# Block products of a chunked recurrence whose backward items write to the other partition half

## The chip, the cores and the metric

One core of a Trainium2 chip runs the whole program as one launch. The metric is the device time of that launch in microseconds (us); smaller is better. Everything is computed in float32.

## The reference

The reference is a two-part network: a first block of two layers (neighbourhood attention, a recurrent mixer, a convolution, then a dense or an expert feed-forward) and a second block of two layers. The change touches one thing in it, the recurrent mixer of the first block. It is computed for 512 tokens, in both directions, with four heads of 64 features. For each head and direction it holds a state matrix `X` (64 x 64) and goes through the tokens:

```
for each token t:   X <- diag(decay_t) X  +  b_t (z_t^T X)  +  k_t v_t^T        (delta-rule update)
                    y_t = X^T r_t                                              (output)
```

The kernel computes it in chunks of 64 tokens. In a chunk the update is a triangular system `(I - L) U = right-hand side`, where `L` (64 x 64, strictly triangular) holds products of the z and b rows. Its inverse is built from matrix products only: the part of `L` inside 16 x 16 blocks, `D`, gives the block inverse `E = (I + D)(I + D^2)(I + D^4)(I + D^8)`, as E1 = I + D, E2 = E1 + D^2 E1, E3 = E2 + D^4 E2, E4 = E3 + D^8 E3. The rest of `L` then gives N = E L', N^2, and `G = (I + N)(I + N^2)`, so that the system is solved by applying E and then G.

## The kernel before, in words

**Data layout.** SBUF and PSUM have 128 partitions; a 64 x 64 matrix fills one half, partitions 0 to 63 or 64 to 127 (`hs`, line 1500). Heads come in two pairs (`hp`), the two heads of a pair in the two halves. With two directions (`d`, 0 forward, 1 backward) and two chunk steps (`j`) a buffer such as `E`, `DD`, `LL`, `D4` holds 8 items side by side, each 64 columns, in both halves: index `i = 4 j + 2 d + hp`. PE's array is used as four quarters of 64 x 64: a matmul reads its operands from one half and writes to one half, so a quarter is a pair (half read, half written).

**A block product** (`products`, lines 1536 to 1541) goes over the 8 items and the two halves and reads and writes the same half. It uses only the two quarters on the diagonal. It is 16 matmuls; each shows in the trace as two pairs of a weight load (PEld) and a matmul, 32 pairs. Other matmuls (`against_zr`, `turned`, `rhs`, `state`, `outputs`) already write backward items to the other half (`time_half`, line 1543), since the backward direction keeps time in the other half.

**Order of the work.** A layer has NG = 4 groups of two chunks. All engines have the order of a group written out by hand, and count steps on three semaphores (`P_`, `V_`, `A_` for PE, VectorE and ScalarE, with the names in the lists of lines 1489 to 1499). In group g the inverse of g is built, in the products p1 to p7, and between them PE does the steps of the group before (s = g - 1): right-hand side (`rhs`), applying E (`solve_blocks`, line 1613), applying G (`solve`, 1618), state update (`state`, 1623) and outputs (`outputs`, 1634), once for each j. Lines 1657 to 1739 are PE's order:

- `dl`, `zb`: L and its transpose (1665, 1671 to 1672), then `rhs(s, 0)`.
- p1 (1677 to 1679): D^2 and its transpose. Then E applied (`w0`), and `kb0` (1683), key products for j = 0.
- p2 (1687 to 1689): D^4, its transpose, D^2 E. Then G applied (`u0`), `kb1` (1693).
- p3 (1697 to 1699): D^8, and D^4 E after E2 is there. Then the state update for j = 0.
- p4 (1705): D^8 E. Then outputs for j = 0 and `rhs(s, 1)`.
- p5 (1712, 1713): N transposed and N. Then `w1`.
- p6 (1722): N^2, then `u1`. p7 (1728): the last product. Then `state(s, 1)`.
- `bs`, `ks`, `vs` (1732, 1733, 1738): transposes by an identity (`turned`, line 1561; matmul at 1566), `outputs(s, 1)`.

ScalarE (lines 1820 to 1855) copies one result of each step out of PSUM (`out`, line 1790, instruction 1792; `rhs_out` 1796, `blocks_out` 1800, `solved` 1804). VectorE (lines 1934 to 1981) masks, copies (line 1913) and adds (line 1910) the others: `e2`, `e3`, `e4` are adds of a PSUM bank to E. Between them it does `taps.some`, multiply-adds of a convolution (line 735) that belong to another mixer and fill its time. `keys_out` (1901) masks the key products `km0`, `km1` (line 1907).

In layer 1 the first two groups need no outputs (`seen`, line 1479), so they have fewer products and narrower ones. In groups 0 and 1 of layer 0 and group 0 of layer 1 `fill_pe` places small matmuls of another part (lines 505 and 522) between the steps. After the fourth group a tail (1740 to 1786) does the steps of that group.

Of the kernel before, what the change touches and what calls it, by code (L numbers as in the profile page):

```python
# [14 lines left out]
P = 128  # L15
# [15 lines left out]
CH = 64  # L31
# [130 lines left out]
def build(nc, parts, xt_in, ct_in, con_in, par1_in, par2_in, lora_in, gate2_in, router_in, bias_in,  # L162
# [1066 lines left out]
    def recurrence(l, us, at, taps, mod, mod_done, mod_here):  # L1229
# [243 lines left out]
        dirs = lambda x: x.rearrange("p (j d hp) t -> p d j (hp t)", j=2, d=2)  # L1473
        step4 = lambda x: x.rearrange("p (d hp) t -> p d (hp t)", d=2)
# [14 lines left out]
        for g in range(NG):  # L1489
            tags_of(pn, ("dl", "zb", "old0", "rhs0", "p1", "w0", "kb0", "p2", "u0", "kb1", "p3", "dx0", "p4", "yx0", "y0", "old1",  # L1490
                         "rhs1", "p5", "w1", "p6", "u1", "p7", "dx1", "bs", "ks", "yx1", "y1", "vs"), g)
            tags_of(vn, ("d", "dt0", "dt1", "l", "e1", "mb0", "mb1", "d2", "km0", "d4", "e2", "km1", "e3", "xa0", "xb0",
                         "e4", "nt", "int", "g", "xa1", "xb1"), g)
            tags_of(an, ("rhs0", "d2t", "w0", "d4t", "u0", "d8", "ya0", "yb0", "rhs1", "n", "w1", "n2", "u1", "bs", "ks", "ya1", "yb1", "vs"), g)
# [26 lines left out]
        def _(pe):  # L1521
# [14 lines left out]
            def products(out, left, right):  # L1536

                for i in range(8):
                    for h in hs:
                        mm = pe.matmul(out[h, i, :], left[h, i, :], right[h, i, :], start=True, stop=True)  # L1540
                return mm
# [65 lines left out]
            def apply(name, region, left, s, j):  # L1607
                for hp, d, q in items():
                    for h in hs:
                        mm = pe.matmul(bank(5 + d)[h, spot(d, region, hp)], left[h, 4 * j + q, :], RH[h, q, :], start=True, stop=True)  # L1610
                mm.then_inc(P_.h, P_.one(f"{name}{j}_{s}"))

            def solve_blocks(s, j):
                pe.wait_ge(V_.h, V_.at(f"e4_{s}"))
                pe.wait_ge(A_.h, A_.at(f"rhs{j}_{s}"))
                apply("w", BLOCKS, E[s % 2], s, j)

            def solve(s, j):
                pe.wait_ge(V_.h, V_.at(f"g_{s}"))
                pe.wait_ge(A_.h, A_.at(f"w{j}_{s}"))  # L1620
                apply("u", RHS_U, GG_, s, j)
# [35 lines left out]
            for g in range(NG):  # L1657
# [54 lines left out]
                products(b8(0), LL, E[g % 2])  # L1712
                products(b8(1), E[g % 2], LL).then_inc(P_.h, P_.one(f"p5_{g}"))
# [4 lines left out]
                pe.wait_ge(V_.h, V_.at(f"km1_{g}"))  # L1718
                pe.wait_ge(A_.h, A_.at(f"n_{g}"))
                if g and seen(s):  # L1720
                    pe.wait_ge(A_.h, A_.at(f"yb0_{s}"))
                products(b8(3), NTb, N1).then_inc(P_.h, P_.one(f"p6_{g}"))
# [66 lines left out]
        def _(act):  # L1789
# [3 lines left out]

            def rhs_out(s, j):
                act.wait_ge(P_.h, P_.at(f"rhs{j}_{s}"))
                act.activation(step4(RH), near(5, RHS_U), ACT.Copy).then_inc(A_.h, A_.one(f"rhs{j}_{s}"))
# [23 lines left out]
            for g in range(NG):  # L1820
# [8 lines left out]
                out("d4t", "p2", g, 1, D4T)  # L1829
# [3 lines left out]
                out("d8", "p3", g, 0, D8)  # L1833
# [5 lines left out]
                out("n", "p5", g, 1, N1)  # L1839
# [3 lines left out]
                out("n2", "p6", g, 3, N2)  # L1843
# [46 lines left out]
        def _(dve):  # L1890
# [4 lines left out]
            of_dir = lambda x, d: x.rearrange("p (j d hp) t -> p d j hp t", j=2, d=2)[:, d]  # L1895
            of_step = lambda x, j, rows: x.rearrange("p (j d hp) w t -> p j d hp (w t)", j=2, d=2)[:, j, :, :, 0:rows * CH]
# [37 lines left out]
            for g in range(NG):  # L1934
                s, rows, e = g - 1, 2 if seen(g) else 1, E[g % 2]
                after(f"dl_{g}")
                mult(dirs(DD), grams, wide("mask_d"), f"d_{g}")
                after(f"zb_{g}")
                for d in range(2):
                    mult(of_dir(DT, d), zr_of(d)[:, :, :, 0, :], per_dir(mdt, d), f"dt{d}_{g}")  # L1940
                mult(dirs(LL), grams, wide("mask_l"), f"l_{g}")
# [11 lines left out]
                copy(D4, b8(0), f"d4_{g}")  # L1953
                add(e, b8(2), e, f"e2_{g}")
# [11 lines left out]
                add(e, b8(2), e, f"e4_{g}")  # L1966
                taps.some(dve, 1)
                after(f"p5_{g}")
                copy(NTb, b8(0), f"nt_{g}")
                add(INT_, b8(0), eye, f"int_{g}")  # L1970
# [1816 lines left out]
```

## Time and profile before

| | before |
|---|---|
| median of 3 runs | 2932.83 us (2929.32 to 2934.77) |
| span of the profiled execution | 2929.3 us |
| PE / PE weight load / VectorE / ScalarE / GpSimd busy | 94% / 78% / 66% / 51% / 3% |
| recurrence, layer 0 (four groups) | about 288.7 to 399 us |
| recurrence, layer 1 (four groups) | about 1064.7 to 1169 us |

The profile gives for every group of instructions the engine, the line of the kernel, the operation and its busy time. PE stands for matmuls, PEld for the weight loads that overlap them, DVE for VectorE, ACT for ScalarE, PEclk for the granted clock as a share of 2.4 GHz. A view by stretches lists for each engine the busy time and, in brackets, the instructions: PE, PEld, DVE, ACT, POOL. In a timeline, neighbouring instructions of the same kind are merged into one row (start, duration of the whole, count), and rows of one engine may overlap by the last instruction's duration. The idle time before a row and its releaser stand in brackets; the releaser "issue" is idle time for which the profile shows no cause. The page gives the span of the execution that was profiled and no other time for it; its span lies at the low end of the three runs.

### The profile page before, as it was taken

To read this page: it belongs to the slowest core of one execution; us is meant where nothing else is said; L and a number is where in the kernel's file an instruction comes from. 1 tells how busy PE (TensorE), PEld (TensorE's weight loads), DVE (VectorE), ACT (ScalarE), POOL (GpSimd) and SP (SyncE) were. 2 spreads that over 40 slices of the span, in tenths; PEclk is the share of its full clock that TensorE was granted. 3 is DMA by queue.
4 is the path that set the end of the run, shared out by engine and by line. 5 is a ranking of instruction groups with operands and counts; after the bars stand their busy time and mean duration, and the time that the engine had idled before them with its cause. 6 is when DMAs were issued, how large, how long until landed. Compare 5 with 4: busy or idle time off the path is not lost.

```text
span 2929.3 us, 50739 instructions
## 1 busy us (share of the span) xinstructions
PE 2739.9 (94%) x21324; PEld 2299.2 (78%) x21324; DVE 1943.8 (66%) x2283; ACT 1481.0 (51%) x1753; POOL 101.6 (3%) x79
## 2 busy tenths in 40 slices
PE   6998888999999978799999999999999889989999
PEld 4875776888768767778778787877877779987999
DVE  3365775322454567578888888888888657665766
ACT  3344243222433433367677777777776445443544
POOL 1100000000012000010000000000000000000000
PEclk9998999999999989899999999999999889998999
DMA  8514101322234230089899898989996424542453
GB/s 318 220 58 172 69 3 62 111 101 87 101 130 155 76 138 4 13 335 373 335 354 348 333 367 336 371 336 349 366 346 258 162 101 175 186 147 87 158 187 117
DMA packets 81796, 581.69 MB, mean 199 GB/s; under 512 B 9272, under 2 KB 11072, under 8 KB 11840
## 3 DMA queue, kind: packets, MB, share of 16 engines
q1 hardware_dynamic: 78336, 571.48, 51.6%
q10 hardware_dynamic: 3264, 7.33, 0.7%
q8 instruction: 155, 2.54, 0.3%
q14 instruction: 41, 0.34, 0.0%
HBM read 577.73 MB, written 1.05 MB: 198 GB/s over the span
## 4 chain that ended last, share of the span: by engine, by line
PE 82%; DVE 8%; ACT 4%; PEld 2%; issue 1%; DMA 1%; PEldq 1%; POOL 0%; POOLq 0%; ACTq 0%; DVEq 0%; SPq 0%
PE banks L2496 20%; PE banks L2520 11%; PE banks L2834 9%; PE banks L1077 8%; PE banks L857 8%; PE banks L1103 3%; PE banks L891 3%; PE banks L1540 3%; PE banks L3160 3%; PEld banks L679 1%; DVE ring_split L307 1%; PE banks L2088 1%; DVE ring_split L2673 1%; PE banks L522 1%; DVE x_buf L2662 1%
## 5 line engine op out<-in xcount | busy, mean ns | idle before, releaser
L2673 DVE TENSOR_TENSOR ring_split<-ring,arena_split 128x2048 fp32r<-128x2048 f32 x336 | 768.3, 2291 | 90.8 <-ACT arena_split L2601 82.6
L2601 ACT ACTIVATE arena_split<-ring 128x2048 fp32r<-128x2048 f32 x336 | 644.3, 1918 | 52.3 <-PE banks L2520 52.2
L307 DVE TENSOR_TENSOR ring_split<-ring,arena_split 128x2048 fp32r<-128x2048 f32 x144 | 339.6, 2360 | 338.0 <-ACT arena_split L301 338.0
L301 ACT ACTIVATE arena_split<-ring 128x2048 fp32r<-128x2048 f32 x144 | 274.4, 1908 | 103.8 <-PE banks L1077 74.0
L2496 PE MATMUL banks<-arena_split 128*128 128x512 f32 x896 | 301.5, 399 | 11.7 <-DVE ring_split L2673 11.7
L2496 PE MATMUL banks<-arena_split,mix_split 128*128 128x512 f32 x896 | 304.1, 401 | 6.4 <-DVE ring_split L2673 6.4
L2520 PE MATMUL banks<-arena_split 128*128 128x512 f32 x896 | 297.2, 392 | 1.0 <-DVE arena_split L2702 1.0
L2496 PEld LDWEIGHTS banks<-arena_split 128*128 128x128 f32 x896 | 169.6, 189 | 49.0 <-DVE ring_split L2673 13.4
L2496 PEld LDWEIGHTS banks<-arena_split,mix_split 128*128 128x128 f32 x896 | 168.3, 188 | 45.0 <-DVE ring_split L2673 8.3
L2520 PEld LDWEIGHTS banks<-arena_split 128*128 128x128 f32 x896 | 168.2, 188 | 43.2 <-issue 4.4
L857 PE MATMUL banks<-mix_split,ring_split 128*128 128x256 f32 x704 | 198.8, 282 | 0.0
L857 PE MATMUL banks<-h_split,arena_split 128*128 128x256 f32 x704 | 197.6, 281 | 0.0
L857 PE MATMUL banks<-mix_split,arena_split 128*128 128x256 f32 x704 | 196.8, 279 | 0.2
L2496 PE MATMUL banks<-ring_split,arena_split 128*128 128x512 f32 x448 | 176.9, 395 | 0.0
L2520 PE MATMUL banks<-ring_split,arena_split 128*128 128x512 f32 x448 | 175.9, 393 | 0.0
L2496 PE MATMUL banks<-ring_split,mix_split 128*128 128x512 f32 x448 | 175.5, 392 | 0.0
L2834 PE MATMUL banks<-mix_split,arena_split 128*128 128x512 f32 (+1 forms) x352 | 138.0, 392 | 11.0 <-DVE h_split L450 9.6
L1077 PE MATMUL banks<-mix_split,arena_split 128*128 128x512 f32 x352 | 139.7, 397 | 7.2 <-DVE h_split L450 7.2
L1077 PE MATMUL banks<-h_split,arena_split 128*128 128x512 f32 x352 | 138.8, 394 | 0.0
L1077 PE MATMUL banks<-mix_split,ring_split 128*128 128x512 f32 x352 | 138.2, 393 | 0.0
L857 PEld LDWEIGHTS banks<-mix_split,arena_split 128*128 128x128 f32 x704 | 132.6, 188 | 2.2 <-issue 1.5
L2834 PE MATMUL banks<-h_split,arena_split 128*128 128x512 f32 (+1 forms) x352 | 132.8, 377 | 0.0
(408 smaller groups left out, 5447.5 us busy)
## 6 DMA issues: line engine op xcount, KB each, us to landing
ring<-parts SPq DMA_DIRECT2D x541, 1024.0 KB, 4.8
arena<-bias ACTq DMA_DIRECT2D x2, 2048.0 KB, 9.5
x_buf<-xt SPq DMA_DIRECT2D x1, 2048.0 KB, 7.8
constants<-con SPq DMA_DIRECT2D x1, 1952.0 KB, 14.5
out<-x_buf ACTq DMA_DIRECT2D x4, 256.0 KB, 2.2
arena<-lora ACTq DMA_DIRECT2D x2, 256.0 KB, 3.4
arena<-gate ACTq DMA_DIRECT2D x2, 256.0 KB, 3.6
arena<-sgw ACTq DMA_DIRECT2D x2, 256.0 KB
```

The source lines that it names most:

```text
L301: act.activation(high[:, m % depth, :], slots[:, n % RING, :], ACT.Copy).then_inc(w_high.h, w_high.one(times))
L307: dve.tensor_tensor(low_slots[:, n % RING, :], slots[:, n % RING, :], high[:, m % high.shape[1], :].bitcast(F32), ALU.subtract).then_inc(w ...
L857: mm = pe.matmul(bk[:, j * 256:(j + 1) * 256], w[:, k, j * P:(j + 1) * P], x[:, k, c0:c0 + 256], start=k == 0 and n == 0, stop=k == KT - 1 ...
L891: mm = pe.matmul(y(t), w[:, j, t * P:(t + 1) * P], h[:, U % 2, j * 256:(j + 1) * 256], start=False, stop=False, skip_group_check=True)
L1077: mm = pe.matmul(o, w[:, k, j * P:(j + 1) * P], x[:, k, :], start=k == 0 and n == 0, stop=k == KT - 1 and n == 2)
L1103: mm = pe.matmul(bank(4 * p + t), w[:, e % 4, c], h[b], start=k == 0 and n == 0, stop=k == n_hid - 1 and n == 2)
L1540: mm = pe.matmul(out[h, i, :], left[h, i, :], right[h, i, :], start=True, stop=True)
L2496: mm = pe.matmul(pair_bank(U), x[:, k, at], w[:, j, :], start=k == 0 and g == 0, stop=k == KT - 1 and g == 2)
L2520: mm = pe.matmul(bank(4 + half), h[:, U % 2, j * P:(j + 1) * P], w[:, j, half * 512:(half + 1) * 512], start=times == 1 and u == 0 and j = ...
L2601: act.activation(high[:, m % 3, :], slots[:, m % RING, :], ACT.Copy).then_inc(wh_ok.h, 1)
L2673: dve.tensor_tensor(low_slots[:, m % RING, :], slots[:, m % RING, :], high[:, m % 3, :].bitcast(F32), ALU.subtract).then_inc(wl_ok.h, 1)
L2834: mm = pe.matmul(o, left, right, start=kk == 0 and n == 0, stop=kk == KT - 1 and n == 2)
```

## The change

Seven of the twelve block products of a group (D^4, its transpose, D^8, N, its transpose, and the two that make E2 and E3) are done by a new function `crossed`. Forward items stay in their half; backward items write to the other half, and forward and backward items go to two neighbouring PSUM banks. The items in the buffers are ordered by direction first (`4 d + 2 j + hp`). For E2 and E3 the sum with E is formed in PSUM by a second matmul with an identity (`plus=True`), since E must move to the other half as well; VectorE then copies instead of adding. D crosses at D^4 and again at D^8, E at E2 and again at E3, so p4 is again an uncrossed product. N and its transpose cross once, so p6 and p7 are uncrossed products of crossed items, and G lies crossed. Applying E crosses the backward items over, applying G crosses them back.

In the order of work `kb1` moves from behind `u0` to behind the state update of j = 0, and waits for the copy of D^8; VectorE's `km1` moves behind `e3` and that state update; PE's waits for `km1` and for the outputs' copy move from p6 to p5; D^4's transpose comes last in p2 and waits for `km0`.

```diff
+        pair = lambda b, k: by_dir(b, b + 2)[:, :, k * 256:(k + 1) * 256].rearrange("p d (i t) -> p d i t", i=4)
+        pair_like = lambda x: x.rearrange("p (d i) t -> p d i t", d=2)
...
+            def crossed(b, k, left, right, plus=False):
+
+                o = [bank(b + d)[:, k * 256:(k + 1) * 256].rearrange("p (i t) -> p i t", i=4) for d in range(2)]
+                for i in range(4):
+                    for w in range(2 if plus else 1):
+                        for d in range(2):
+                            for h in hs:
+                                to = hs[1 - hs.index(h)] if d else h
+                                mm = pe.matmul(o[d][to, i, :], eye[h, 0, :] if w else left[h, 4 * d + i, :], right[h, 4 * d + i, :],
+                                               start=w == 0, stop=w == int(plus))
                 return mm
...
-            def apply(name, region, left, s, j):
+            def apply(name, region, left, s, j, from_crossed):
                 for hp, d, q in items():
                     for h in hs:
-                        mm = pe.matmul(bank(5 + d)[h, spot(d, region, hp)], left[h, 4 * j + q, :], RH[h, q, :], start=True, stop=True)
+                        of, to = (time_half(h, q), h) if from_crossed else (h, time_half(h, q))
+                        mm = pe.matmul(bank(5 + d)[to, spot(d, region, hp)], left[of, 4 * d + 2 * j + hp, :], RH[of, q, :],
+                                       start=True, stop=True)
...
-                products(b8(0), D2T, D2)
-                products(b8(1), D2, D2T)
-                products(b8(2), D2, E[g % 2]).then_inc(P_.h, P_.one(f"p2_{g}"))
+                crossed(0, 0, D2T, D2)
+                crossed(0, 1, D2, E[g % 2], plus=True)
+                pe.wait_ge(V_.h, V_.at(f"km0_{g}"))
+                crossed(2, 0, D2, D2T).then_inc(P_.h, P_.one(f"p2_{g}"))
                 if g:
                     solve(s, 0)
-                pe.wait_ge(V_.h, V_.at(f"km0_{g}"))
-                against_zr(kt, g, 1).then_inc(P_.h, P_.one(f"kb1_{g}"))
...
-                products(b8(0), D4T, D4)
+                crossed(2, 0, D4T, D4)
                 pe.wait_ge(V_.h, V_.at(f"e2_{g}"))
-                products(b8(1), D4, E[g % 2]).then_inc(P_.h, P_.one(f"p3_{g}"))
+                crossed(0, 0, D4, E[g % 2], plus=True).then_inc(P_.h, P_.one(f"p3_{g}"))
                 if g:
                     state(s, 0)
+                pe.wait_ge(A_.h, A_.at(f"d8_{g}"))
+                against_zr(kt, g, 1).then_inc(P_.h, P_.one(f"kb1_{g}"))
...
-                products(b8(2), D8, E[g % 2]).then_inc(P_.h, P_.one(f"p4_{g}"))
+                products(b8(0), D8, E[g % 2]).then_inc(P_.h, P_.one(f"p4_{g}"))
...
                 pe.wait_ge(V_.h, V_.at(f"e4_{g}"))
-                products(b8(0), LL, E[g % 2])
-                products(b8(1), E[g % 2], LL).then_inc(P_.h, P_.one(f"p5_{g}"))
+                if g and seen(s):
+                    pe.wait_ge(A_.h, A_.at(f"yb0_{s}"))
+                pe.wait_ge(V_.h, V_.at(f"km1_{g}"))
+                crossed(2, 0, LL, E[g % 2])
+                crossed(0, 0, E[g % 2], LL).then_inc(P_.h, P_.one(f"p5_{g}"))
...
-                copy(D4, b8(0), f"d4_{g}")
-                add(e, b8(2), e, f"e2_{g}")
+                copy(pair_like(D4), pair(0, 0), f"d4_{g}")
+                copy(pair_like(e), pair(0, 1), f"e2_{g}")
+                taps.some(dve, 1)
+                after(f"p3_{g}")
+                copy(pair_like(e), pair(0, 0), f"e3_{g}")
+                if g:
+                    state(s, 0)
                 after(f"kb1_{g}")
                 keys_out(g, 1, rows)
                 taps.some(dve, 1)
-                after(f"p3_{g}")
-                own()
-                add(e, b8(1), e, f"e3_{g}")
-                if g:
-                    state(s, 0)
-                taps.some(dve, 1)
```

## Rows read from the trace of the kernel before

**Rows 1.** The page: span, busy times, PE's instruction queue, shares of the chain by line.

```profile
span 2929.3 us, 50739 instructions
PE 2739.9 (94%) x21324; PEld 2299.2 (78%) x21324; DVE 1943.8 (66%) x2283; ACT 1481.0 (51%) x1753; POOL 101.6 (3%) x79
...
q8 instruction: 155, 2.54, 0.3%
...
PE banks L2496 20%; PE banks L2520 11%; PE banks L2834 9%; PE banks L1077 8%; PE banks L857 8%; PE banks L1103 3%; PE banks L891 3%; PE banks L1540 3%; PE banks L3160 3%; PEld banks L679 1%; DVE ring_split L307 1%; PE banks L2088 1%; DVE ring_split L2673 1%; PE banks L522 1%; DVE x_buf L2662 1%
```

**Rows 2.** Stretches: length, then busy us (count) by engine, clock, DMA share, GB/s.

```profile
317.60:344.60 27.00, 24.31 (x868) 22.78 (x868) 23.01 (x48) 7.35 (x18) 0.00 (x0) 0.98 0.02 4
344.60:371.30 26.70, 24.26 (x916) 22.98 (x918) 22.24 (x40) 9.28 (x20) 0.00 (x0) 1.00 0.02 5
1091.30:1114.70 23.40, 20.46 (x768) 19.22 (x768) 16.84 (x38) 6.68 (x15) 0.00 (x0) 1.00 0.02 5
```

**Rows 3.** Timeline of group 1 of layer 0, p2 to p4.

```profile
323.39 2.88 PEld L1540 LDWEIGHTS banks<-arena 64*64 64x64 f32 x96
...
323.61 1.41 DVE L735 SCALAR_TENSOR_TENSOR mix_buf<-arena,par,mix_buf 128x512 f32<-128x512 f32 x2
...
326.18 0.55 PEld L1610 LDWEIGHTS banks<-arena 64*64 64x64 f32 x16
...
326.45 0.69 DVE L1913 COPY arena<-banks 128x512 f32<-128x512 f32 x1 [1.44 <-PE banks L1540]
...
327.06 0.68 DVE L1910 TENSOR_TENSOR arena<-banks,arena 128x512 f32<-128x512 f32 x1
327.20 1.95 PEld L1540 LDWEIGHTS banks<-arena 64*64 64x64 f32 x64
...
330.32 1.01 PEld L1540 LDWEIGHTS banks<-arena 64*64 64x64 f32 x32 [0.71 <-DVE arena L1910]
...
330.83 0.49 DVE L1930 TENSOR_TENSOR arena<-arena 128x128 f32<-128x128 f32 x2
...
331.25 0.55 PEld L1641 LDWEIGHTS banks<-arena 64*64 64x64 f32 x16
```

**Rows 4.** Stops named "issue": timeline, stretches between stops, and the queues from 343.48.

```profile
339.84 0.13 PEld L1630 LDWEIGHTS banks<-arena 64*64 64x64 f32 x1 [0.24 <-issue]
339.85 1.06 PEld L1566 LDWEIGHTS banks<-constants,h_buf 64*64 64x64 f32 x64
...
343.49 0.21 PEld L1566 LDWEIGHTS banks<-constants,arena 64*64 64x64 f32 x8 [1.17 <-issue]
...
369.71 0.21 PEld L1665 LDWEIGHTS banks<-h_buf,arena 64*64 64x64 f32 x8 [0.86 <-issue]
...
339.83:343.48 3.65, 2.55 (x128) 2.27 (x127) 3.48 (x8) 1.53 (x4) 0.00 (x0) 1.00 0.03 7
366.36:369.70 3.34, 2.56 (x130) 2.27 (x127) 3.25 (x7) 2.30 (x6) 0.00 (x0) 1.00 0.02 5
1164.97:1169.05 4.08, 2.77 (x127) 2.38 (x126) 1.28 (x4) 3.15 (x6) 0.00 (x0) 1.00 0.01 4
343.48:369.70 26.22, 23.70 (x888) 22.28 (x888) 22.97 (x48) 8.20 (x20) 0.00 (x0) 1.00 0.02 4
...
q8 instruction: 7, 0.11, 1.8%
```

**Rows 5.** Timeline of the same group: an operation on four quarters.

```profile
332.46 0.33 PEld L1588 LDWEIGHTS banks<-arena 64*64 64x64 f32 x16
```

**Rows 6.** First groups: two stops (timeline), then both groups by stretches.

```profile
301.52 0.66 PEld L1540 LDWEIGHTS banks<-arena 64*64 64x64 f32 x19 [1.31 <-issue]
...
314.42 0.20 PEld L1566 LDWEIGHTS banks<-constants,h_buf 64*64 64x64 f32 x6 [2.72 <-issue]
...
288.70:317.60 28.90, 21.48 (x648) 18.20 (x652) 20.44 (x34) 5.16 (x9) 0.00 (x0) 0.96 0.57 230
1064.67:1091.30 26.63, 21.09 (x612) 19.88 (x612) 15.75 (x36) 4.53 (x8) 0.00 (x0) 0.81 0.12 51
```

More of the change, by code:

```diff
@@ L1489, in recurrence @@
         for g in range(NG):
-            tags_of(pn, ("dl", "zb", "old0", "rhs0", "p1", "w0", "kb0", "p2", "u0", "kb1", "p3", "dx0", "p4", "yx0", "y0", "old1",
+            tags_of(pn, ("dl", "zb", "old0", "rhs0", "p1", "w0", "kb0", "p2", "u0", "p3", "dx0", "kb1", "p4", "yx0", "y0", "old1",
                          "rhs1", "p5", "w1", "p6", "u1", "p7", "dx1", "bs", "ks", "yx1", "y1", "vs"), g)
-            tags_of(vn, ("d", "dt0", "dt1", "l", "e1", "mb0", "mb1", "d2", "km0", "d4", "e2", "km1", "e3", "xa0", "xb0",
+            tags_of(vn, ("d", "dt0", "dt1", "l", "e1", "mb0", "mb1", "d2", "km0", "d4", "e2", "e3", "xa0", "xb0", "km1",
                          "e4", "nt", "int", "g", "xa1", "xb1"), g)
@@ L1620, in solve @@
                 pe.wait_ge(A_.h, A_.at(f"w{j}_{s}"))
-                apply("u", RHS_U, GG_, s, j)
+                apply("u", RHS_U, GG_, s, j, True)
             def state(s, j):
@@ L1717, in _ @@
                 pe.wait_ge(V_.h, V_.at(f"nt_{g}"))
-                pe.wait_ge(V_.h, V_.at(f"km1_{g}"))
                 pe.wait_ge(A_.h, A_.at(f"n_{g}"))
-                if g and seen(s):
-                    pe.wait_ge(A_.h, A_.at(f"yb0_{s}"))
-                products(b8(3), NTb, N1).then_inc(P_.h, P_.one(f"p6_{g}"))
+                products(b8(4), NTb, N1).then_inc(P_.h, P_.one(f"p6_{g}"))
                 if g:
@@ L1792, in out, with pair_out @@
                 act.activation(o, b8(b), ACT.Copy).then_inc(A_.h, A_.one(f"{name}_{g}"))
+            def pair_out(name, of, g, b, o):
+                act.wait_ge(P_.h, P_.at(f"{of}_{g}"))
+                act.activation(pair_like(o), pair(b, 0), ACT.Copy).then_inc(A_.h, A_.one(f"{name}_{g}"))
             def rhs_out(s, j):
@@ L1828, in _ @@
                 fill_act(act, g, "p1")
-                out("d4t", "p2", g, 1, D4T)
+                pair_out("d4t", "p2", g, 2, D4T)
                 if g:
@@ L1832, in _ @@
                 fill_act(act, g, "p2")
-                out("d8", "p3", g, 0, D8)
+                pair_out("d8", "p3", g, 2, D8)
                 fill_act(act, g, "p3")
@@ L1838, in _ @@
                 fill_act(act, g, "p4")
-                out("n", "p5", g, 1, N1)
+                pair_out("n", "p5", g, 0, N1)
                 if g:
@@ L1842, in _ @@
                 fill_act(act, g, "p5")
-                out("n2", "p6", g, 3, N2)
+                out("n2", "p6", g, 4, N2)
                 if g:
@@ L1936, in _ @@
                 after(f"dl_{g}")
-                mult(dirs(DD), grams, wide("mask_d"), f"d_{g}")
+                mult(own_dirs(DD), grams, wide("mask_d"), f"d_{g}")
                 after(f"zb_{g}")
                 for d in range(2):
-                    mult(of_dir(DT, d), zr_of(d)[:, :, :, 0, :], per_dir(mdt, d), f"dt{d}_{g}")
-                mult(dirs(LL), grams, wide("mask_l"), f"l_{g}")
+                    mult(own_dir(DT, d), zr_of(d)[:, :, :, 0, :], per_dir(mdt, d), f"dt{d}_{g}")
+                mult(own_dirs(LL), grams, wide("mask_l"), f"l_{g}")
                 own()
@@ L1957, in _ @@
                 taps.some(dve, 1)
-                after(f"p3_{g}")
-                own()
-                add(e, b8(1), e, f"e3_{g}")
-                if g:
-                    state(s, 0)
-                taps.some(dve, 1)
                 after(f"p4_{g}")
                 own()
-                add(e, b8(2), e, f"e4_{g}")
+                add(e, b8(0), e, f"e4_{g}")
                 taps.some(dve, 1)
                 after(f"p5_{g}")
-                copy(NTb, b8(0), f"nt_{g}")
-                add(INT_, b8(0), eye, f"int_{g}")
+                copy(pair_like(NTb), pair(2, 0), f"nt_{g}")
+                add(pair_like(INT_), pair(2, 0), eye_pair, f"int_{g}")
                 taps.some(dve, 2)
```

6 lines of the change are left out of this document (5 added, 1 removed).

## The prediction

> **What bounds the kernel now.** The page's shares come first: TensorE (PE) is busy 94% of the span, and the chain that ended last runs over its lines; the block products of line 1540 are 3% of it, some 88 us [rows 1]. So a shorter PE stage here can shorten the kernel, unless another wait takes its place. The busy time by stretches shows two full groups of layer 0 at 27.0 and 26.7 us and one of layer 1 at 23.4 us; in layer 0 PE is busy 24.3 us of a group and VectorE (DVE) 22 to 23 us [rows 2] (the second stretch ends inside the next group, so it counts more loads). DVE is a close second, so not all that PE saves can show. There are eight groups, four in each layer.
>
> The timeline of one group of layer 0 is the next view [rows 3]. The reader is to see three kinds of piece: products that PE runs back to back (96 weight loads from 323.39, and the next line starts at 326.18), waits for a copy to land (0.71 us before p4 at 330.32), and DVE's convolution taps, each pair 1.41 us, which sit between the copies.
>
> The last view decides this forecast: stops of PE whose releaser is "issue", that is nothing the profile shows. There is one of 0.24 us before 339.84 and one of 1.17 us before 343.49 [rows 4]. Between the two PE ran 127 pairs of a weight load and a matmul and took 3.65 us, though it was busy only 2.3 to 2.6 us. From 366.37 to 369.71 it is 127 pairs again and 3.34 us, ending in a stop of 0.86 us, and in layer 1 126 pairs and 4.08 us [rows 4]. From stop to stop, 343.49 to 369.71, there are 888 pairs, one short of 7 times 127, and the instruction queue q8 moved 7 packets [rows 4]; its packets are 2.54 MB over 155, 16.4 KB each [rows 1]. I read this so: one packet carries some 256 PE instructions (127 pairs, two instructions each, and the waits among them), and a new packet serves PE every 3.34 to 4.08 us at best, mostly 3.4 to 3.6. I take 3.5 us, or 27 ns for a pair. A product on two quarters issues at 2.79/96 = 29 ns for a pair [rows 3], just under that ceiling, which is why only the stretches at the end of a group hit it.
>
> **The change part by part.**
>
> *Five plain crossed products* (D4, D4T, D8, N, NT). A product is 16 matmuls, 32 pairs in the trace. On two quarters it takes 0.93 us (2.79/3) [rows 3]. On all four the trace has another operation with the same shape and the same order over directions and halves, line 1566: 64 loads in 1.06 us, of which the last lasts 0.13, so 14.7 ns a pair and 0.47 us for 32 [rows 4]. That saves 0.46 each, 2.3 a group.
>
> *Two crossed products with E added on PE* (E2, E3): 64 pairs at 14.7 ns, 0.94 us, against 0.93. Nothing saved, but 64 more pairs a group. DVE's add becomes a copy of the same size: 0.68 us against 0.69 [rows 3], nothing.
>
> *Applying the inverse,* four times a group: 16 pairs in 0.55 us now (line 1610), 0.33 us where four quarters are used (line 1588) [rows 3, 5]. That is 0.2 each, 0.8 a group.
>
> So PE's own work falls by 3.1 us a group, about 24 us in all. How much shows, if instructions are always there, I walk along the group. p2: 128 pairs, 1.87 us against 2.79, gain 0.9; DVE is done with km0 and its taps at 325.02, before the product would land, so nothing takes that back. The way to p3: before, solve and kb1 cover the copy of D4 (326.18 to 327.20, 1.02 us); after, kb1 is gone from there but PE waits for the copy all the same, gain 0. D8 takes 0.47, but E3 must wait for the copy of E2, 0.61 behind that of D4: 0.3 gained of 0.46. p4: E3's copy no longer queues behind km1 and taps, so the wait of 0.71 us before p4 [rows 3] shrinks to 0.4, gain 0.3; kb1 (16 pairs, 0.4 us) fits into that wait, its new wait for d8 included. But km1 now stands on DVE behind e3 and the state update (0.69, some 0.4 for an add of half the size, 0.49 and 0.69 us), and the outputs and the right-hand side queued on PE wait for it: 0.5 lost. p5: 0.93 gained, less 0.15 since nt then comes behind two taps. p6, p7 and the turned products: nothing; their moved waits (km1, yb0) are done by then. Together 1.8 us a group, **14 us** in all. No transfer, SyncE or GpSimd step is moved.
>
> *Instructions.* The same trace says they are not always there. A layer 0 group has 864 pairs (868 loads in the window less 4 of another line [rows 2]) and would have 928. With some 18 waits in the code that is 7.3 packets, 25.6 us at 3.5 each, against 26.9 measured; in layer 1's first groups 768 pairs become 832, 6.6 packets, 23.0 us against 23.4. So even with no other wait the eight groups could gain only 5 us. And packets are not evenly used. From p2 to the end of p4 the new order wants 128+16+96+32+16+32 = 320 pairs, 2.5 packets or 8.75 us; a packet that lies ready at its start makes up part of it, and I take 8.4. Now it is 7.86 us (323.39 to 331.25). That is 0.5 slower where the walk above had gained 1.0. The km1 wait costs nothing here, since PE stands in the same place for instructions. The rest of the group keeps about 0.7 of its 0.8, as the stop at its end (1.17 us before 343.49) only starts earlier. Net 0.2 a group: **−1.4 us**.
>
> *The first group of layer 0* runs while weights stream in (DMA share 0.57 [rows 6]); its stops for instructions are 1.31 and 2.72 us [rows 6], so a packet takes longer there, some 5 us. 64 more pairs are half a packet: between 0 and +2.8 us on top, and I take **+2.5**, since all its long stops are of this kind.
>
> *The tail* of each layer has four applies with ScalarE between them: 0.2 each where PE is late, at most 1.6 over both layers; half of it lies beside convolution work. **−0.6**.
>
> Sum: −1.4 + 2.5 − 0.6 = +0.5 us. The profiled execution spans 2929.3 us; the runs shown are 2929.32 to 2934.77, median 2932.83, so the profile is 0.12% under the median. I forecast **2933.3 us**, no change that can be told (0.2%, 5.9 us, is about what a measurement of this kernel can tell).
>
> Now two rules of the Trainium skill. The rows show PE stopped for up to 1.17 us at exact multiples of 256 instructions with almost no other DMA about [rows 4]. "Runtime: NRT & Kernel Launch", Instruction fetch mechanics, says blocks of 256 instructions are refilled ahead, and that fetching is hidden because instructions issue more slowly than they arrive. The block size agrees with the trace; the hiding does not. By that rule the sum would be rival 1's. "TensorE: Matmul & The Clock Gate", section "Wait — 56ns, not 53.3ns?", says starts of matmuls never come closer than about 25 ns however small they are. By that rule crossing gains next to nothing and the added pairs cost in full, rival 3; the trace has 14.7 ns.
>
> **The rivals.**
>
> *Rival 1: instructions keep up.* Then the 14 us of the walk and 0.6 of the tail show: 2932.8 − 14.6 = **2918.2 us**. For it: most of the 256-instruction blocks pass without a stop today. Against it: they do so at 29 ns a pair, and all dense stretches at 15 ns show a stop or a thinning. A ceiling of 3.3 us rather than 3.5 gives half of it, about −5.
>
> *Rival 2: the ceiling is lower than I take it,* in the stretch from p2 to p4. Price: at 3.8 us a packet it takes 2.5 × 3.8 = 9.5 less what lies ready, 9.1, so 1.2 us more than now, of which 0.5 comes back later; with eight groups and the first one's 2.5 it is +8, **2941 us**. It decides from about 3.6 us a packet. For it: the 3.65 and 4.08 us intervals; against: 3.34.
>
> *Rival 3: crossed products do not overlap* as line 1566 does, since there one operand is a constant. At 29 ns a pair the two long products cost 0.93 more each, and nothing is gained: 8 × 1.9 = +15, **2948 us**. Against it: line 1588 multiplies data by data and reaches 0.33 us for 16 pairs [rows 5].
>
> **How the numbers follow.** The forecast, instructions as the ceiling near 3.5: 0.62. Rival 1 with its halfway case 0.17; rival 2: 0.17; rival 3: 0.04. Faster by over 0.2% takes rival 1 and the edge of the forecast, 0.18; slower by over 0.2% takes rivals 2 and 3 and its other edge, 0.22; within, 0.60. The range runs from 2921 us, which holds the halfway case and part of rival 1, to 2942 us, rival 2's end; the ends beyond hold under 0.2. PE's clock is at the upper level (1.00) in the full groups and lower in the first group of layer 1 (0.81 [rows 6]); I see nothing that moves it, and 1 us either way is inside the range.
>
> **What would show it.** Right: plain crossed products at about 15 ns a pair; "issue" stops inside p3, p4 and p5 of nearly every group, at distances of 256 PE instructions and 3.4 to 3.7 us; about 4 more packets on q8 in all; groups of 26.5 and 23 us; PEld counts 64 higher a group. Wrong: groups of 25 and 21 us with no new stop (rival 1); intervals of 3.8 us and more (rival 2); 29 ns a pair on the new line (rival 3); or PE waits for km1 before the outputs larger than 0.5 us with instructions at hand.

## The result and the profile after

The changed kernel takes 2940.47 us (median of 20 runs, 2934.3 to 2947.77), beside 2932.75 for the kernel before in the same comparison (20 runs, 2920.94 to 2938.67). The ratio is 1.0026, 95% interval 1.0018 to 1.0034. That is 7.7 us slower, just more than the 0.2% bound, while PE's busy time fell by 10.9 us.

First the page of the changed kernel: span, busy times, PE's instruction queue, the chain by engine.

```profile
span 2943.7 us, 51759 instructions
...
PE 2729.0 (93%) x21836; PEld 2282.7 (78%) x21836; DVE 1941.7 (66%) x2283; ACT 1480.5 (50%) x1753; POOL 101.4 (3%) x79
...
q8 instruction: 159, 2.61, 0.4%
...
PE 82%; DVE 8%; ACT 4%; issue 2%; PEld 2%; DMA 1%; PEldq 1%; POOL 0%; POOLq 0%; ACTq 0%; DVEq 0%; SPq 0%
```

Against [rows 1] there are 512 more pairs of a weight load and a matmul, 64 in each of eight groups, and q8 moved 159 packets where it moved 155. DVE and ScalarE do what they did. The profiled execution is one of the slower ones (2943.7 us, 14.4 over the profile of before, where the medians differ by 7.7), so lengths are read stage by stage.

The first three groups of each layer, from group start to group start, by the same columns as [rows 2]:

```profile
289.21:316.66 27.45, 20.22 (x673) 16.33 (x676) 19.33 (x33) 4.45 (x8) 0.00 (x0) 0.88 0.61 242
316.66:345.52 28.86, 22.86 (x947) 21.17 (x942) 23.54 (x42) 7.53 (x18) 0.00 (x0) 0.94 0.02 4
345.52:371.82 26.30, 21.48 (x941) 19.45 (x937) 21.74 (x47) 7.08 (x17) 0.00 (x0) 1.00 0.02 4
1073.15:1095.94 22.79, 16.92 (x641) 15.63 (x645) 15.29 (x32) 4.07 (x7) 0.00 (x0) 0.85 0.09 34
1095.94:1119.77 23.83, 17.43 (x848) 16.24 (x843) 16.66 (x41) 6.64 (x14) 0.00 (x0) 1.00 0.02 4
1119.77:1145.32 25.55, 19.32 (x847) 17.33 (x841) 18.70 (x41) 6.53 (x14) 0.00 (x0) 1.00 0.02 4
```

And the same six in the kernel before, cut at the same places of the code:

```profile
288.70:316.33 27.63, 20.21 (x609) 17.04 (x612) 20.44 (x34) 4.57 (x8) 0.00 (x0) 0.98 0.59 240
316.33:343.72 27.39, 24.78 (x878) 23.28 (x875) 22.20 (x40) 7.43 (x18) 0.00 (x0) 0.96 0.02 4
343.72:368.63 24.91, 23.11 (x878) 21.83 (x874) 21.66 (x47) 7.14 (x17) 0.00 (x0) 1.00 0.02 5
1064.67:1090.52 25.85, 20.35 (x577) 19.29 (x580) 15.19 (x32) 4.07 (x7) 0.00 (x0) 0.80 0.13 53
1090.52:1113.70 23.18, 20.47 (x784) 19.23 (x779) 16.39 (x40) 6.54 (x14) 0.00 (x0) 1.00 0.02 5
1113.70:1137.35 23.65, 21.12 (x783) 19.90 (x777) 18.45 (x41) 6.54 (x14) 0.00 (x0) 1.00 0.02 4
```

The reader is to see two things. In the four full groups PE is busy 1.6 to 3.0 us less and the group is 0.65 to 1.9 us longer: what PE no longer works, it waits. And the first groups did not get slower. The end of the recurrence is marked in the timeline by the first reciprocal behind it, first in the changed kernel, then in the kernel before:

```profile
435.79 0.20 DVE L2209 RECIPROCAL arena<-arena 128x8 f32<-128x8 f32 x1 [1.20 <-ACT arena L2168]
...
1201.29 0.18 DVE L2209 RECIPROCAL arena<-arena 128x4 f32<-128x4 f32 x1 [0.58 <-ACT arena L2168]
```

```profile
429.01 0.20 DVE L2186 RECIPROCAL arena<-arena 128x8 f32<-128x8 f32 x1 [1.20 <-ACT arena L2145]
...
1191.60 0.18 DVE L2186 RECIPROCAL arena<-arena 128x4 f32<-128x4 f32 x1 [0.58 <-ACT arena L2145]
```

From the last group's start to there it is 63.97 us against 60.38 in layer 0 and 55.97 against 54.25 in layer 1. Together: +5.4 in the full groups, −3.2 in the first ones, +5.3 in the last ones with the tail, so +7.5 us inside the recurrence; the other 6.9 us of this execution lie outside, where the code is the same. This is near the difference of the medians, but it is no proof, since single executions differ too. The traces of e4 and e6 below, whose medians cannot be told from the kernel before's, have 2.9 and 4.3 us more than this trace of before in the same four full groups, and e6 has 64.16 us from the last group's start of layer 0 to the reciprocal. The medians and the experiments carry the verdict; the traces show where the time goes.

Where in a group? The stretch from the first weight load of p2 to the end of p4, in the four full groups of the changed kernel:

```profile
325.14:333.16 8.02, 6.58 (x321) 5.99 (x321) 6.50 (x13) 1.47 (x3) 0.00 (x0) 1.00 0.02 4
351.65:360.67 9.02, 6.64 (x320) 6.01 (x321) 7.59 (x14) 1.60 (x4) 0.00 (x0) 1.00 0.01 4
1101.44:1110.73 9.29, 5.80 (x320) 5.52 (x320) 5.14 (x13) 1.70 (x4) 0.00 (x0) 1.00 0.02 5
1125.68:1135.24 9.56, 6.62 (x319) 5.90 (x320) 6.34 (x14) 1.59 (x4) 0.00 (x0) 1.00 0.02 3
```

It holds the 320 pairs forecast and takes 8.97 us on the mean, of which PE is busy 6.4. Before, the same stretch was 7.86, 7.85, 7.76 and 7.76 us with 256 pairs. The timeline of group 2 of layer 0 shows what fills the rest:

```profile
356.20 0.26 PEld L1554 LDWEIGHTS banks<-arena 64*64 64x64 f32 x11 [0.73 <-issue]
...
360.03 0.71 PEld L1543 LDWEIGHTS banks<-arena 64*64 64x64 f32 x21 [0.99 <-issue]
...
364.07 0.67 PEld L1554 LDWEIGHTS banks<-arena 64*64 64x64 f32 x40 [0.86 <-issue]
```

Three stops for instructions in a row, 3.83 and 4.04 us apart; the stretches between them hold 129 and 127 pairs. Beside them PE waits for copies, 0.70 us before 354.93 and 0.38 before 358.18. In [rows 4] such stops stood at the end of a group; now they stand inside it as well. Counted in 256 instructions, eight blocks start from 345.28 to 371.01, and five of them start with an "issue" stop. From 323.81 to 372.22 the packets on q8 start 3.72 us apart on the mean.

The added identity pairs are no dearer for the array than the others. At the start of the same stretch in group 1 they alternate with products, eight pairs each, and eight start every 0.11 to 0.12 us, 15 ns a pair:

```profile
325.72 0.21 PEld L1554 LDWEIGHTS banks<-arena,constants 64*64 64x64 f32 x8
325.84 0.21 PEld L1554 LDWEIGHTS banks<-arena 64*64 64x64 f32 x8
325.95 0.21 PEld L1554 LDWEIGHTS banks<-arena,constants 64*64 64x64 f32 x8
```

### The profile page after: what moved, and what is told of

Its sections match the earlier page's. It is cut to its first block, busy times and chain, and to the rows that moved or that the text cites. A ratio compares the mean times of both kernels' runs of the same rounds, so it can differ in the third digit from the quotient of the medians.

```text
span 2943.7 us, 51759 instructions
## 1 busy us (share of the span) xinstructions
PE 2729.0 (93%) x21836; PEld 2282.7 (78%) x21836; DVE 1941.7 (66%) x2283; ACT 1480.5 (50%) x1753; POOL 101.4 (3%) x79
## 3 DMA queue, kind: packets, MB, share of 16 engines
HBM read 577.73 MB, written 1.05 MB: 197 GB/s over the span
## 4 chain that ended last, share of the span: by engine, by line
PE 82%; DVE 8%; ACT 4%; issue 2%; PEld 2%; DMA 1%; PEldq 1%; POOL 0%; POOLq 0%; ACTq 0%; DVEq 0%; SPq 0%
PE banks L2519 20%; PE banks L2543 11%; PE banks L2857 9%; PE banks L1077 8%; PE banks L857 8%; PE banks L1103 3%; PE banks L891 3%; PE banks L3183 3%; PE banks L1543 2%; PE banks L1554 1%; PE banks L2111 1%; PEld banks L679 1%; DVE ring_split L307 1%; DVE ring_split L2696 1%; PE banks L522 1%
```

## The experiments

Times are medians, ratios are against the kernel before on the same chip with their 95% intervals. In these comparisons the kernel before has 2935.0 to 2937.9 us, not 2932.75, so differences and ratios are to be compared with the expectations, not their absolute times. "Instruction theory": PE is given a block of 256 instructions, 127 or 128 pairs, every 3.5 to 4 us at best, and what it does in its quarters matters only beyond that. "Array theory": the quarters and the waits for copies set the time.

**e1: the same instructions on two quarters.** In the changed kernel:

```diff
-                                to = hs[1 - hs.index(h)] if d else h
+                                to = h
...
-                        of, to = (time_half(h, q), h) if from_crossed else (h, time_half(h, q))
+                        of, to = h, h
```

> The changed kernel with every crossed matmul and both applies written to the half they are read from, so that only two quarters are used; number and order of PE instructions, copies and waits are the changed kernel's. What is computed for backward items of the recurrence is another thing. Instruction theory (256 PE instructions are served every 3.7 us, 29 ns a pair, whatever the quarters): a two-quarter pair costs 29 ns, just what the instructions allow, so this is only a little slower than the changed kernel, +2 to +8 us (2942 to 2949). Array theory (the crossing pays in full, and the loss lies in the moved waits): PE's own work grows by 14 ns on 160 pairs of plain products, 128 of E2 and E3 and 64 of the applies, 5.0 us a group: +25 to +40 us against the changed kernel.

Measured: 2952.88 us, ratio 1.0051 (1.0037 to 1.0066). That is some 7 us over the changed kernel, inside what the instruction theory allowed (+2 to +8) and far from the array theory's +25 to +40. Taking the four quarters away costs only 7 us although PE's busy time rises by 32 (2761.0 us). Where the expectation speaks of other sums, it is wrong: every item stays in its half, and the sums are complete.

**e2: without the identity products.**

```diff
-                crossed(0, 1, D2, E[g % 2], plus=True)
+                crossed(0, 1, D2, E[g % 2])
...
-                crossed(0, 0, D4, E[g % 2], plus=True).then_inc(P_.h, P_.one(f"p3_{g}"))
+                crossed(0, 0, D4, E[g % 2]).then_inc(P_.h, P_.one(f"p3_{g}"))
```

> The changed kernel without the 32 identity matmuls a group (64 pairs, 128 PE instructions) that add E to D^2 E and D^4 E; E is left out of these sums, all else as in the changed kernel. Instruction theory: half a packet less a group, 1.9 us, so -12 to -15 us against the changed kernel: 2926 to 2929, below the kernel before. Array theory: 64 pairs at 14.7 ns, 0.94 us a group, at most -7.5 us: 2933 or more.

Measured: 2923.89 us, ratio 0.9958 (0.9943 to 0.9973), so 12 us under the kernel before. E is left out of the sums E2 and E3. Two full groups, one of each layer:

```profile
314.79:340.33 25.54, 21.46 (x879) 19.76 (x875) 21.94 (x39) 7.53 (x18) 0.00 (x0) 0.95 0.02 5
...
1088.01:1109.91 21.90, 18.14 (x780) 16.92 (x775) 16.10 (x36) 6.54 (x14) 0.00 (x0) 0.91 0.02 5
```

The instruction theory had −12 to −15 for the group's 64 pairs against the changed kernel, the array theory at most −7.5; it is −20 (12 under the kernel before, which the changed one is 8 over). So both were too low, and the 64 pairs cost at least what they cost as instructions. What makes the other 5 us is not shown.

**e3: only N, its transpose and the applies cross.** The order and the products up to p4 are those of the kernel before; nothing is added on PE.

```diff
-                crossed(0, 0, D2T, D2)
-                crossed(0, 1, D2, E[g % 2], plus=True)
-                pe.wait_ge(V_.h, V_.at(f"km0_{g}"))
-                crossed(2, 0, D2, D2T).then_inc(P_.h, P_.one(f"p2_{g}"))
+                products(b8(0), D2T, D2)
+                products(b8(1), D2, D2T)
+                products(b8(2), D2, E[g % 2]).then_inc(P_.h, P_.one(f"p2_{g}"))
...
                 crossed(2, 0, LL, E[g % 2])
                 crossed(0, 0, E[g % 2], LL).then_inc(P_.h, P_.one(f"p5_{g}"))
```

> Only N, its transpose and the applies of the inverse cross; p2, p3, p4 and the order of kb1 and km1 are those of the kernel before. As many PE instructions as before; PE's own work falls by 0.9 us a group in p5 and 0.8 in the applies. Instruction theory: the kernel before already averages one packet in 3.75 us, so the stops at the group's end grow by nearly as much as the products shrink: 0 to -4 us against the kernel before (2929 to 2933). Array theory: 1.2 us a group beyond waits show: -8 to -10 us (2923 to 2925).

Measured: 2926.51 us, ratio 0.9966 (0.9955 to 0.9978), 10 us faster than the kernel before. Here the array theory (−8 to −10) was right and the instruction theory (0 to −4) wrong: the blocks of the kernel before are not all full of pairs at 29 ns, some are long because of their work and waits, and there shorter work shows. The two groups that answer to those of e2 are 26.33 and 22.27 us (27.39 and 23.18 before).

**e4: the order alone.** kb1 and km1 of the kernel before are moved to where the change has them:

```diff
-                pe.wait_ge(V_.h, V_.at(f"km0_{g}"))
-                against_zr(kt, g, 1).then_inc(P_.h, P_.one(f"kb1_{g}"))
...
+                pe.wait_ge(V_.h, V_.at(f"km0_{g}"))
+                pe.wait_ge(A_.h, A_.at(f"d8_{g}"))
+                against_zr(kt, g, 1).then_inc(P_.h, P_.one(f"kb1_{g}"))
```

> The kernel before with the moved steps alone: kb1 behind the state update and waiting for the copy of D^8, km1 behind e3 and the state update on VectorE. No product crosses, as many PE instructions as before. Instruction theory: within 3 us of the kernel before, either way. Wait theory (the outputs and the right-hand side stand behind km1): +0.5 to +1 us a group, +4 to +8 us, all of the change's loss.

Measured: 2937.71 us, ratio 1.0006 (0.9995 to 1.0017), that is −1.5 to +5 us. The moved steps cost nothing that can be told, but the lower end of the wait theory (+4) is not shut out by this run alone. e2 and e11 have the same moved steps and are faster than the kernel before, so the order alone is not what made the changed kernel slow. The waits that the change moves from p6 to p5 are not in e4.

**e5 and e6: fewer instructions by a merge.** D2·D2T and D2·E have the same left operand and become one product of 128 columns, in e3's kernel (e5) and in the kernel before (e6):

```diff
-                products(b8(1), D2, D2T)
-                products(b8(2), D2, E[g % 2]).then_inc(P_.h, P_.one(f"p2_{g}"))
+                for i in range(8):
+                    for h in hs:
+                        mm = pe.matmul(both(i, h), D2[h, i, :], d2t_and_e(g % 2)[h, :, i * CH:(i + 1) * CH], start=True, stop=True)
+                mm.then_inc(P_.h, P_.one(f"p2_{g}"))
```

> The kernel of e3 (only N, its transpose and the applies cross), with one further edit: D2*D2T and D2*E have the same weights, so they become one product of 128 columns, 16 matmuls in place of 32, or 32 pairs of a weight load and a matmul in the trace in place of 64. A group of layer 0 so has 832 pairs where e3 and the kernel before have 864, and PE's multiplications are the same ones. The copies wait for each other in one more place (E2 on DVE waits for the copy of D4T on ScalarE). Instruction theory (PE gets 256 instructions, 127 pairs, in 3.75 us at best, so a pair costs 29 ns whatever it does): 32 pairs fewer are a quarter of a packet, 0.9 us a group or 7 us in all, so 0.993 to 0.995 of the kernel before (some 2918 us where that is 2933). Array theory (what PE does in its quarters sets the time): two quarters stream the same columns as before, so the merge saves only the loads, and the added wait eats it: no different from e3, 0.996 to 0.998.

> The kernel before with the merge of e5 and nothing else: no product crosses halves. It tells how much of the gain of leaving out instructions is there without any crossing. Instruction theory: the kernel before stands just above the ceiling (3.83 us for 256 PE instructions over its full groups, against 3.75), so taking 32 pairs away helps only where PE stands for instructions: between -3 and -8 us, ratio 0.9972 to 0.999. Array theory: the two products take the same columns in the same two quarters: 0.999 to 1.001, or slower by the added wait.

Measured: e5 2931.38 us, ratio 0.9987 (0.9973 to 1.0001); e6 2937.58 us, ratio 1.0005 (0.9996 to 1.0014). Both missed what the instruction theory expected, and e5 is no better than e3, rather worse. The timeline of e5 has a reason that can be seen:

```profile
347.09 1.01 PEld L1547 LDWEIGHTS banks<-arena 64*64 64x64 f32 x32
348.02 1.73 PEld L1711 LDWEIGHTS banks<-arena 64*64 64x64 f32 x32
```

A pair of 128 columns takes 1.73/32 = 54 ns where two of 64 take 58: PE's time is the same, with half the instructions in it. From the stop before 342.50 to the next one for instructions before 358.22 there are four blocks of 256 instructions, this product in one of them, in 15.72 us, 3.93 each. There PE stands for its own work and for copies, and fewer instructions do not help; the gain does not come back later either, so blocks do not seem to be stored up far ahead. So a saved pair is worth its 29 ns only where PE stands for instructions; a sum of pairs over a whole group, as in the prediction and in these two expectations, is the wrong account. Whether the added wait of one copy for the other took the rest is not tested.

**e7 to e10: the price of a pair by itself.** Before group 2 of layer 0 of the kernel before, 1024 more pairs go into bank columns that nothing reads:

```diff
+                if l == 0 and g == 2:
+                    for _ in range(32):
+                        for hp, d, q in 2 * list(items()):
+                            for h in hs:
+                                pe.matmul(bank(d)[time_half(h, q), 256 + hp * CH:256 + hp * CH + CH], bt[h, q, 0:CH], eye[h, 0, 0:CH], start=True, stop=True)
```

That is e7. In e8 the output is `bank(0)[h, ...]`, two quarters; in e9 the moving operand is `eye[h, 0, 0:8]`; in e10 the first loop is `with pe.Fori(0, 32)`, a loop of the engine.

> The kernel before with 1024 more pairs of a weight load and a 64-column matmul (2048 PE instructions, 8 packets of 256) put before group 2 of layer 0, written out straight, over all four quarters, into bank columns that nothing reads. They wait for nothing, so their length is the price of the pair itself. Instruction theory: 8 packets at 3.75 us, 28 to 31 us, with a stop named issue at the same place of every 256 instructions. Array theory: 14.7 ns a pair as in the short four-quarter stretches, 15 us.

> The same 1024 pairs, straight, in two quarters instead of four (each half of the rows to its own half of the columns). Both theories: about 29 ns a pair, 29.8 us. So the instruction theory says that it is as long as the probe over four quarters, the array theory that it is twice as long.

> The probe over four quarters with 8 moving columns instead of 64 in each matmul. Instruction theory: no shorter, 28 to 31 us. Array theory: no longer than the probe of 64 columns, 15 us or less.

> The probe over four quarters with its 1024 pairs as 32 passes of a loop over 32 pairs (64 instructions), instead of written out. Instruction theory, if the loop's body stays in the sequencer and is not read again: 14.7 ns a pair, 15 us, plus what a jump costs 32 times, and q8 moves 8 packets fewer than in the straight probe. If the body is read again at each pass, it is no shorter than 30 us. Array theory: the same 15 us as the straight one.

Measured, each in one run beside 2935.0 us for the kernel before: 2960.65, 2964.22, 2967.19 and 2957.05 us. Runs of the kernel before lie up to 18 us apart, so single runs cannot rank the probes: e10 is only 3.6 us under e7, though its probe is over 11 us shorter. The stretches of the traces are what is compared. The timeline of e7 (four quarters, straight):

```profile
348.10 1.96 PEld L1665 LDWEIGHTS banks<-constants,h_buf 64*64 64x64 f32 x128 [1.77 <-issue]
351.56 1.96 PEld L1665 LDWEIGHTS banks<-constants,h_buf 64*64 64x64 f32 x128 [1.50 <-issue]
355.01 1.96 PEld L1665 LDWEIGHTS banks<-constants,h_buf 64*64 64x64 f32 x128 [1.50 <-issue]
358.46 1.96 PEld L1665 LDWEIGHTS banks<-constants,h_buf 64*64 64x64 f32 x128 [1.50 <-issue]
362.47 1.96 PEld L1665 LDWEIGHTS banks<-constants,h_buf 64*64 64x64 f32 x128 [2.04 <-issue]
366.19 1.96 PEld L1665 LDWEIGHTS banks<-constants,h_buf 64*64 64x64 f32 x128 [1.77 <-issue]
370.20 1.96 PEld L1665 LDWEIGHTS banks<-constants,h_buf 64*64 64x64 f32 x128 [2.04 <-issue]
```

Then the stretch, and its instruction queue:

```profile
348.10:370.20 22.10, 12.57 (x769) 11.75 (x769) 0.00 (x0) 0.00 (x0) 0.00 (x0) 1.00 0.02 4
```

```profile
q8 instruction: 6, 0.10, 1.6%
```

This is the mechanism with nothing else about: 128 pairs in 1.96 us (15 ns each), then a stop of 1.50 to 2.04 us, six times; six packets, 22.10/6 = 3.68 us each, 29 ns a pair. No other transfer uses the queues at that time (DMA share 0.02) and no other engine works. The prediction had taken 3.5. All 1024 pairs take 29.6 us (344.61 to 374.21), inside the 28 to 31 of the instruction theory.

The timelines of e8 (two quarters), e9 (8 columns) and e10 (loop), a fence each:

```profile
352.58 3.81 PEld L1665 LDWEIGHTS banks<-constants,h_buf 64*64 64x64 f32 x128 [0.19 <-issue]
```

```profile
356.04 3.50 PEld L1665 LDWEIGHTS banks<-constants,h_buf 64*64 64x64 f32 x128 [0.49 <-issue]
```

```profile
344.98 17.83 PEld L1665 LDWEIGHTS banks<-constants,h_buf 64*64 64x64 f32 x1021
```

And stretches of several blocks of e8 and of e9:

```profile
348.58:368.32 19.74, 19.52 (x640) 18.98 (x640) 0.00 (x0) 0.00 (x0) 0.00 (x0) 1.00 0.01 4
```

```profile
348.03:370.95 22.92, 21.46 (x768) 20.98 (x768) 0.00 (x0) 0.00 (x0) 0.00 (x0) 0.50 0.02 4
```

On two quarters a block holds 3.81 us of work and the stop shrinks to 0.19; it takes 19.74/5 = 3.95 us. On four quarters the block holds half the work and takes 7% less time, where the array theory had half; the expectation that e7 and e8 are equally long missed by those 7%. The 8-column probe ran at the lower of PE's clock levels (granted clock 0.50, after a stop of 1.50 us and 107 pairs of 8 columns), so its pairs are 27 ns long and it tells little; at 22.92/6 = 3.82 us a block it is no shorter than e7, as the instruction theory had it. The loop decides: the same 1024 pairs as in e7, without a stop, in 17.83 us, 17 ns each, and q8 moves 155 packets, those of the kernel before, where the straight probes have 163. The engine is able to run at 17 ns a pair; it is handed new instructions at 29.

**e11: the changed kernel without the 64 pairs, all sums complete.** E comes in through the left operand:

```diff
-                crossed(0, 1, D2, E[g % 2], plus=True)
+                pe.wait_ge(V_.h, V_.at(f"d2i_{g}"))
+                crossed(0, 1, D2I, E[g % 2])
...
-                crossed(0, 0, D4, E[g % 2], plus=True).then_inc(P_.h, P_.one(f"p3_{g}"))
+                crossed(0, 0, D4I, E[g % 2]).then_inc(P_.h, P_.one(f"p3_{g}"))
...
                 copy(D2, b8(1), f"d2_{g}")
+                own()
+                add(D2I, D2, eye, f"d2i_{g}")
...
-                copy(pair_like(e), pair(0, 1), f"e2_{g}")
+                own()
+                add(D4I, D4, eye, f"d4i_{g}")
```

> The changed kernel, computing all it should, without its 64 additional pairs a group: E is not added by an identity product but by the left operand, (D2 + I) times E and (D4 + I) times E, so a group has 864 pairs, as before, and five products more cross. VectorE forms D2 + I and D4 + I (two instructions of some 0.69 us), and one copy of its own, that of E2, goes to ScalarE (0.6 us), behind the copies of D4 and D4T. Instruction theory in its present form (a block of 256 PE instructions lasts as long as its own work and waits, and never less than 3.5 to 4.0 us): the groups fall to about those of e2, which left E out, 25.5 to 26 us in layer 0 and 22 to 23 in layer 1, less what the added copies make late: 15 to 20 us under the changed kernel, ratio to before 0.9945 to 0.9975, about e3's or a little under it. If it was the crossing itself, or the moved waits, that made the changed kernel slow, and not the 64 pairs: as the changed kernel, 1.001 to 1.004. If VectorE is the bound (two more instructions, one fewer: 0.7 us a group): up to 6 us of the gain is lost, 0.997 to 0.9995.

Measured: 2926.78 us, ratio 0.9968 (0.9955 to 0.998), 9 us under the kernel before and some 17 under the changed one: 2.1 us for each group's 64 pairs, or 33 ns a pair. The stretch from p2 to the end of p4:

```profile
321.53:328.75 7.22, 5.54 (x257) 4.92 (x256) 7.05 (x14) 2.07 (x4) 0.00 (x0) 1.00 0.02 5
346.94:354.58 7.64, 5.95 (x256) 5.15 (x256) 7.47 (x14) 2.19 (x5) 0.00 (x0) 1.00 0.02 4
1090.96:1098.72 7.76, 5.64 (x257) 4.82 (x257) 5.97 (x14) 2.19 (x5) 0.00 (x0) 1.00 0.02 4
1114.60:1122.38 7.78, 5.84 (x256) 5.01 (x256) 6.49 (x14) 2.19 (x5) 0.00 (x0) 1.00 0.02 4
```

With 256 pairs it is 7.60 us on the mean, two blocks of 3.8, though PE works only 5.7 us in it; the kernel before worked 7.3 us and took 7.81. So crossing the products of p2 and p3 saves PE 1.6 us of work there, and 0.2 us of time. The array theory's price for the 64 pairs was at most 7.5 us in all; 17 us, with the identity pairs themselves running at 15 ns in the trace, leaves the instructions as the cause. At e7's 29 ns they would be 15 us, near enough given the intervals.

e3 and e11 both beat the kernel before and the changed one. They are equal within their intervals; e3 is the simpler.

## Why the prediction was right, and where it was off

The median of 2940.5 us lies in the range, at the place of rival 2 (2941 us), not at the forecast of 2933.3. The ceiling by instructions was the right mechanism. Its size was taken too low, and the way it was summed over a group was wrong. The nearness to 2941 is partly luck: rival 2 reached +8 by +0.7 in each of eight groups and +2.5 in the first one, where the traces have +1.35 on the mean in the full groups, −0.2 and −3.1 in the first ones and +5.3 in the last ones, which may not belong to the change.

- *Crossed products overlap.* Right: the 64 loads of line 1554 at p5 (335.19) took 1.05 us, as line 1566's 1.06 [rows 4]. Rival 3 is out.
- *64 pairs more a group, 320 between p2 and p4, some 4 packets more on q8.* Right to the pair (x320; 159 against 155).
- *PE's own work −3.1 us a group.* PE's busy time is 1.6, 1.8, 1.9 and 3.0 us less in the four full groups; why mostly less than 3.1 is not shown. As forecast, it does not show in the time. The walk's 1.8 us a group adds no term for the applies; e3, which crosses only p5 and the applies, gains some 1.25 us a group, where the walk had 0.8 for p5.
- *The km1 wait costs nothing.* Nearly. In two of the four full groups PE waits for it, 0.31 us before 333.16 and 0.40 before 1110.73; e4 shows no cost of the order that can be told.
- *"I take 3.5 us, or 27 ns for a pair."* This is the term that was off (3.5/127 is nearer 28 ns). The straight probe has 3.68 us with PE idle in over 40% of it; the text had said that rival 2 decides from about 3.6, and it does. The intervals of 3.34 and 3.65 us [rows 4] from which 3.5 was drawn were single ones; e7 has 3.45 three times in a row and then 4.01, 3.72 and 4.01, so a mean over several in a row was needed.
- *"A packet that lies ready makes up part of it, and I take 8.4"* for p2 to p4. Measured 8.97 (8.02 to 9.56), beside rival 2's 9.1.
- *"0.7 of 0.8 kept"* in the rest of the group. Not kept: the rest of the four full groups is 0.2 us longer on the mean (+1.31, +0.23, −0.88, +0.10). The account by sums of packets missed this: a block lasts as long as its own work and waits, or as the delivery, whichever is longer, and a short block hands little on to the next. e5 and e6 failed by the same account.
- *First group of layer 0, +2.5.* Not seen: 27.45 us against 27.63. But single traces can't price this group: e4, with the pairs of the kernel before, has 25.51 us there, and the traces of e7 to e10, which are the kernel before up to that point, have 28.7 to 29.0.
- *Tail −0.6.* Not seen: last group and tail together +3.6 and +1.7. The trace shows part of it as clock: over 378.20:382.00 the granted clock is 0.50, and 63 loads of line 1543 take 3.48 us, where 64 of line 1540 took 1.94 in the same place before. That this comes with the change is not shown: e6, which crosses nothing, has 64.16 us in layer 0 where the changed kernel has 63.97 and the kernel before 60.38. e6 and the changed kernel have a granted clock of 0.92 there, the kernel before 1.00.
- *Rival 1, instructions keep up.* Out. It is what the Trainium skill says in "Runtime: NRT & Kernel Launch", Instruction fetch mechanics, where fetching hides behind slower issue. The probe shows stops of 1.50 to 2.04 us at each 256 instructions, so the measurement decides against it here.

e11 shows the two sides of the change apart: crossing alone, which takes 23 us off PE's busy time (2716.5 us), is worth 9 us, and the 64 pairs a group cost 17. Of those 9 us the crossing of p5 and the applies gives all that can be told, since e3 has them alone.

## What to carry to other kernels

Where small matmuls are written out straight, count instructions beside array time: here a block of 256 PE instructions came every 3.45 to 4.0 us, 3.7 on the mean, so in a long run of them a pair of a weight load and a matmul costs 29 ns even where the array could do it in 15. An addition moved from VectorE to PE as identity matmuls is then not free; put it into an operand, or into a copy that is made anyway. The sign in a profile is "issue" stops at equal counts of instructions, here 256; count per block, not per stage, since a block that is long for another reason is not helped by fewer instructions.

## What the hardware showed that was not expected

- Most of the time between two blocks is not the transfer of a packet. In e7 a packet on q8 takes 0.92 to 1.23 us, the next block starts 1.3 to 1.5 us after its end, and the next packet starts another 1.0 to 1.7 us later: 3.45 to 4.01 us in all, with the transfer queues otherwise idle. What fills the rest is not shown. In none of the 13 traces do two packets of q8 start closer than 3.23 us.
- A loop of 64 PE instructions is not delivered again: in e10 no packet moved on q8 from 346.94 to its end at 362.7, and a pair cost 17 ns, 2 more than straight within a block.
- A pair with 128 moving columns on two quarters costs 54 ns in e5, against 29 with 64.
- A low granted clock in one group did not decide the order of the kernels: e2, the fastest, has a granted clock of 0.52 over the 27.46 us of its first group of layer 1, where the changed kernel has 0.85.
